# A conditioned mixer and 32 experts on one core: another order of weight loads, x scaled earlier, and products moved in TensorE's order

## The reference, cut to what matters

```
cond = silu(c)
mod = cond @ w_ada + b_ada
sh1, sc1, gt1, sh2, sc2, gt2 = split(mod, 6)
h = rms_norm(x, g_pre_mix) * (1 + sc1) + sh1
q, k, v, u, g_att, g_ssm = split(h @ w_in)
att = moba_attention(q, k, v, rel_bias) @ w_att_out
y = gelu(s5_ssm(u, ...))
glu_v, glu_g = split(y @ w_glu)
ssm = (glu_v * sigmoid(glu_g)) @ w_ssm_out
y = (sigmoid(g_att) * att + sigmoid(g_ssm) * ssm) @ w_out
x = x + gt1 * rms_norm(y, g_post_mix)
h = rms_norm(x, g_pre_ffn) * (1 + sc2) + sh2
x = x + gt2 * rms_norm(moe_ffn(h, ...), g_post_ffn)
```

## Time and profile before

| | |
|---|---|
| median of 3 runs | 1281.6 us (1278.81 to 1281.63) |
| the profiled execution, own time | 1276.95 us |
| its span | 1274.9 us |
| TensorE busy, share of the span | 1161.4 us, 91% |
| VectorE, ScalarE, GpSimd busy | 282.7, 166.4, 133.6 us |
| read from HBM | 463.72 MB |
| mean granted clock of TensorE | 0.955 |

### The profile page before, as it was taken

One profiled execution on the slowest core, in us unless ns is written; L12 is line 12 of the kernel. 1 busy time (PEld: TensorE's weight loads), 2 busy tenths in 40 slices (PEclk: granted clock), 3 DMA queues, 4 the chain that ended last, 5 costly groups with the idle time before them and its releaser, 6 DMA issues.

```text
span 1274.9 us, 16975 instructions
## 1 busy us (share of the span) xinstructions
PE 1161.4 (91%) x6973; PEld 593.1 (47%) x6973; DVE 282.7 (22%) x613; ACT 166.4 (13%) x360; POOL 133.6 (10%) x200
## 2 busy tenths in 40 slices
PE   5999999998999999989999899999799998899874
PEld 3665776856445444344543344443344442345332
DVE  3663784323210211101111111011002111011102
ACT  2201111202101111011011011011110110010001
POOL 4450776120000000000000000000000000000000
PEclk9998999997998999989999799999899999899887
DMA  9789434193899999999999999999999999999995
GB/s 350 249 315 353 165 129 171 66 388 132 363 379 422 419 422 422 420 421 404 421 420 421 421 421 414 420 421 420 420 415 416 420 421 421 420 414 421 420 421 238
DMA packets 88643, 465.93 MB, mean 365 GB/s; under 512 B 12451, under 2 KB 13608, under 8 KB 39412
## 3 DMA queue, kind: packets, MB, share of 16 engines
q1 hardware_dynamic: 86740, 460.27, 89.0%
q0 software_dynamic: 1568, 4.46, 1.1%
q10 hardware_dynamic: 256, 0.09, 0.0%
HBM read 463.72 MB, written 3.16 MB: 366 GB/s over the span
## 4 chain that ended last, share of the span: by engine, by line
PE 49%; SPq 30%; DMA 16%; issue 3%; DVE 1%; ACT 1%; ACTq 0%; POOL 0%; DVEq 0%; POOLq 0%
SPq L556 29%; DMA ring_w<-in_w_exp_out 10%; PE psum L762 9%; PE psum L1072 7%; PE psum L1175 4%; PE psum L1068 4%; PE psum L775 3%; PE psum L1077 3%; DMA ring<-in_w_ada 3%; PE psum L1004 2%; PE psum L1177 2%; PE psum L822 1%; PE psum L1209 1%; PE psum L1104 1%; PE psum L1207 1%
## 5 line engine op out<-in xcount | busy, mean ns | idle before, releaser
L1072 PE MATMUL psum<-ring_w,xe 128*64 128x512 f32 x960 | 210.6, 594 | 2.6 <-DMA ring_w<-in_w_exp_in 2.5
L1914 DVE TENSOR_SCALAR row_a<-psum 128x512 f32<-128x512 f32 (+1 forms) x37 | 22.1, 597 | 619.2 <-PE psum L1091 447.5
L1077 PE MATMUL psum<-ring_w,xe 128*32 128x256 f32 x1536 | 109.5, 432 | 37.8 <-DMA ring_w<-in_w_exp_in 34.2
L1072 PEld LDWEIGHTS psum<-ring_w,xe 128*64 128x64 f32 x960 | 67.0, 137 | 138.0 <-issue 128.0
L1177 PE MATMUL psum<-ring_w,aT 128*64 128x512 f32 x480 | 116.6, 609 | 5.0 <-DMA ring_w<-in_w_exp_out 4.5
L1068 PE MATMUL psum<-ring_w,xe 128*128 128x512 f32 x256 | 114.1, 598 | 3.9 <-DMA ring_w<-in_w_exp_in 3.9
L607 POOL TENSOR_SCALAR small<-small 128x1 f32<-128x1 f32 x6 | 1.5, 253 | 979.9 <-ACT row_g L1532 959.8
L1077 PEld LDWEIGHTS psum<-ring_w,xe 128*32 128x32 f32 x1536 | 49.4, 120 | 94.8 <-DMA ring_w<-in_w_exp_in 57.5
L762 PE MATMUL psum<-hT,ring 128*128 128x256 f32 x384 | 90.7, 393 | 1.6 <-DMA ring<-in_w_in 1.6
L1465 ACT ACTIVATE row_b<-row_a 128x512 f32<-128x512 f32 (+1 forms) x37 | 20.5, 554 | 535.2 <-DVE row_a L1914 535.2
L762 PEld LDWEIGHTS psum<-hT,ring 128*128 128x128 f32 x384 | 73.6, 195 | 16.2 <-issue 4.4
(11 more groups left out here) (312 smaller groups left out, 1026.5 us busy)
## 6 DMA issues: line engine op xcount, KB each, us to landing
ring_w<-in_w_exp_in SPq DMA_DIRECT2D x256, 1024.0 KB, 25.9
ring_w<-in_w_exp_out SPq DMA_DIRECT2D x128, 1024.0 KB, 26.5
ring<-in_w_ada SPq DMA_DIRECT2D x12, 2048.0 KB, 15.7
ring<-in_w_in SPq DMA_DIRECT2D x8, 2048.0 KB, 15.8
ring<-in_w_out SPq DMA_DIRECT2D x2, 2048.0 KB, 11.2
ring<-in_w_glu SPq DMA_DIRECT2D x1, 2048.0 KB, 7.9
ring<-in_w_att_out SPq DMA_DIRECT2D x1, 2048.0 KB, 8.3
ring<-in_w_ssm_out SPq DMA_DIRECT2D x1, 2048.0 KB, 10.4
```

What stands on the lines that cost most here:

```text
L1072: mm = pe.matmul(bank[b][64 * n:64 * n + 64, :], rows[:, k, :], w[:, FF * b + 512 * n:FF * b + 512 * n + 512], start=k == 0, stop=False, t ...
L1077: mm = pe.matmul(bank[0][32 * n:32 * n + 32, 256 * b:256 * b + 256], rows[:, k, :], w[:, FF * b + 256 * n:FF * b + 256 * n + 256], start=k ...
```

## The change

SP issues the mixer's blocks in an order of its own, ISSUE. Slots are still given by MIX, in which glu and ao change places. u comes as two transfers of 1 MB; the second is issued two blocks later and counts on another semaphore, which TensorE waits for before u's second half. ScalarE's squares of x, and VectorE's scalings, stand ahead of the parameters' chain. TensorE turns x before its first weight sum. The sums of sc1b and sh1b run inside u's first half, `inputs_to_states(0)` before the columns of sc2b, and wo0's first product waits for the merged pieces one by one.

```
-MIX = [..., "gt2a", "glu", "gt2b", "ao", "so", "wo0", "wo1"]
+MIX = [..., "gt2a", "ao", "gt2b", "glu", "so", "wo0", "wo1"]
+
+ISSUE = ["sc1a", "sh1a", "u", "sc1b", "sh1b", "u_rest", "q", "k", "gt1b", "gt1a", "sh2a", "v", "sc2a", "sh2b", "ga0", "sc2b",
+         "ga1", "gs0", "gs1", "gt2a", "ao", "gt2b", "glu", "so", "wo0", "wo1"]
...
-            for n, name in enumerate(MIX):
+            for name in ISSUE:
+                if name == "u_rest":
+                    sp.dma_start(slot(MIX.index("u") % MIX_SLOTS, 8)[:, 4:8, :],
+                                 source("u")[0][D // 2:D, :].rearrange("(k p) n -> p k n", p=P)).then_inc(stored, 16)
+                    continue
+                n = MIX.index(name)
...
-                if name == "sh2a":
+                if name == "sc2a":
                     sp.wait_ge(bias_out, 16)
...
+                if name == "u":
+                    sp.dma_start(slot(s, k)[:, 0:4, :], src[0:D // 2, :].rearrange("(k p) n -> p k n", p=P)).then_inc(slot_in[s], 16)
+                    continue
...
-            for name, s in (("ao", 1), ("so", 2), ("wo0", 3), ("wo1", 0)):
+            for name, s in (("glu", 1), ("so", 2), ("wo0", 3), ("wo1", 0)):
...
+                    if merged and k % 2 == 0:
+                        pe.wait_ge(merged_ready, k // 2 + 1)
...
-            ada_parts(0)
             for a in range(TT):
                 pe.wait_ge(normed, a + 1)
                 for k in range(KD):
+                    if a == 0 and k == 6:
+                        pe.wait_ge(vcol_ready, 1)
...
+            ada_parts(0)
             ada_columns(0)
...
                     for n in (2, 3):
-                        ada_parts(n)
                         ada_columns(n)
...
+                        if half == 0 and b == 1 and m == 1:
+                            ada_parts(2)
+                            ada_parts(3)
+                        if half and b == 0 and m == 0:
+                            pe.wait_ge(stored, 16)
...
             ada_parts(9)
+            inputs_to_states(0)
             ada_columns(9)
...
-            pe.wait_ge(merged_ready, 4)
...
-            for name in ("wo0", "wo1"):
-                tokens(name, 0, aoT)
+            tokens("wo0", 0, aoT, merged=True)
+            tokens("wo1", 0, aoT)
...
+            act.wait_ge(x_in, 16 * TT)
+            for n in range(TT):
+                act.activation(junk, xs[:, n, :], ACT.Square, accum_out=ss[:, n:n + 1]).then_inc(squares, 1)
+                act.wait_ge(squares, n + 1)
+
             act.wait_ge(vcol_ready, 1)
...
+            def normal(a):
+                dve.wait_ge(rstd_ready, a + 1)
+                ts(xs[:, a, :], xs[:, a, :], rstd[:, a:a + 1], None, ALU.mult).then_inc(normed, 1)
+
             dve.memset(b_rows, 0.0).then_inc(b_rows_clear, 1)
+            normal(0)
             dve.wait_ge(vec_in, 160)
...
             dve.tensor_copy(vcol, bank[3][:, 0:108]).then_inc(vcol_ready, 1)
+            normal(1)
```

More of the change, by code:

```diff
@@ L54 @@
 MIX = ["sc1a", "sh1a", "u", "sc1b", "sh1b", "q", "gt1a", "k", "gt1b", "v", "sh2a", "sh2b", "sc2a", "sc2b",
-       "ga0", "ga1", "gs0", "gs1", "gt2a", "glu", "gt2b", "ao", "so", "wo0", "wo1"]
+       "ga0", "ga1", "gs0", "gs1", "gt2a", "ao", "gt2b", "glu", "so", "wo0", "wo1"]
+ISSUE = ["sc1a", "sh1a", "u", "sc1b", "sh1b", "u_rest", "q", "k", "gt1b", "gt1a", "sh2a", "v", "sc2a", "sh2b", "ga0", "sc2b",
+         "ga1", "gs0", "gs1", "gt2a", "ao", "gt2b", "glu", "so", "wo0", "wo1"]
 ADA = ["sc1a", "sh1a", "sc1b", "sh1b", "gt1a", "gt1b", "sh2a", "sh2b", "sc2a", "sc2b", "gt2a", "gt2b"]
@@ L121 @@
 FILLS = []
-for name in MIX[:MIX.index("glu")] + ["ao", "glu", "so"]:
+for name in MIX[:MIX.index("gt2a")] + ["ao", "glu", "so"]:
     if name in ("glu", "ao"):
@@ L588, in _ @@
                 sp.dma_start(out[0, a * P:(a + 1) * P, :], xs[:, a, :]).then_inc(stored, 16)
-            sp.wait_ge(stored, 16 * TT)
+            sp.wait_ge(stored, 16 * TT + 16)
         @block.gpsimd
@@ L766, in features, with tokens @@
                 mm.then_inc(fill_done, 1)
-            def tokens(name, a, lhs):
+            def tokens(name, a, lhs, merged=False):
                 s = MIX.index(name) % MIX_SLOTS
@@ L915, in _ @@
             for h in range(HEADS):
-                inputs_to_states(h)
+                if h:
+                    inputs_to_states(h)
                 if 0 < h < HEADS - 1:
@@ L1334, in copy_ada @@
                 act.activation(ada_acc[:, n % 2, :], bank[ADA_BANK[n]], ACT.Copy).then_inc(ada_copied, 1)
[L1336 to L1339, removed]
             for half in range(2):
@@ L1577, in _ @@
             V.do(ts(x_scale_b, x_scale_b, 1.0, None, ALU.add))
-            for a in range(TT):
-                dve.wait_ge(rstd_ready, a + 1)
-                ts(xs[:, a, :], xs[:, a, :], rstd[:, a:a + 1], None, ALU.mult).then_inc(normed, 1)
             chain(tt(m1, rho, ec, ALU.mult))
```

## The result

The changed kernel takes 1271.8 us (median of 12 runs, 1267.8 to 1278.3), the kernel before, on the same chip, 1278.3 us (12 runs, 1274.2 to 1281.6). The ratio is 0.9956 [0.9938, 0.9974]: 5.6 us or 0.44% faster. The profiled executions differ by 5.9 us (own times 1271.08 and 1276.95). The ratios go by executions in the usual state; only one of those reported here was not, at 6416 us, of the kernel with gt1a second.

A forecast was written before the change was run, and what follows sets the result against it. The expert weights' stream bounds a rigid expert stage, so the mixer's gain decides: - 5.8 + 1.1 (sh2a's wait) + 5.2 + 4.8 + 1.5 = 6.8 us won, 1281.6 to 1274.8; range 1268 to 1282.

The forecast's parts named there:

- What bounds it: Expert stage: limited by the expert weights' stream and rigid, so the end moves one to one with the experts' order.
- Start and u in halves: Mixer's start: u at 24.3 instead of 26.21, 1.9 won; with u halved, 3 to 5 us won by q's first half.
- The new order of loads: Behind q: gt1a lands at 64.0, its sum 2.8 late, plus 3.0 of slow clock; 5.8 us lost by q's end.
- sc2b "about when wanted": Late mixer load: issued at v's end near 110, lands 8 later, about when wanted, as before; no term in the sum.
- The first heads: From last weight sum to the first head's product: 9.3 us instead of 14.5, 5.2 won, of which 3.08 is clock.
- ao, wo0: Late mixer: ao's 3.02 wait and slow group go, 4.8 won; wo0's 1.51 wait goes whole, 1.5 won.
- rival 1: gt1a less late, landing at 61.8, 2.4 lost; sum 10.2 won, 1271.4 us; chance 0.16.
- Rival 2: Clock takes most: gt1a at 65, 5 us lost clock, slow first head; 2.1 won, 1279.5; chance 0.24 with rival 4.
- Rival 3: Queue behind q runs at 254 GB/s, gt1a at 72 to 74; sum -3.2, 1284.8 us; chance 0.10.
- Rival 4: Waits move to other names, such as sc2b, without being removed; of rival 2's size; chance 0.24 with rival 2.

The follow-up runs named there:

- the kernel with gt1a second: The changed kernel with loads issued q, gt1a, k, gt1b instead of q, k, gt1b, gt1a: 0.9917 of the kernel before.
- the late scaling: Squares and scalings of x late as before: on the changed kernel 0.9974; on the one with gt1a second and sc2b ahead of ga0 0.9916.
- Writing by partition: Bias rows' write with 128 partitions outermost: with gt1a second 0.9873, the same with u as one transfer 0.9891, on the changed kernel alone 0.9952.
- the repeat: The changed kernel run again, unchanged: 0.9956 of the kernel before, its profiled execution 1276.6 us.
- gt1a third: The changed kernel with loads issued q, k, gt1a, gt1b instead of q, k, gt1b, gt1a: 0.9953 of the kernel before.
- sc2b ahead of ga0: The kernel with gt1a second, with sc2b issued before ga0 instead of after it: 0.9892 of the kernel before.

## Why the prediction was right

It forecast 6.8 us, 1274.8; measured are 5.6 us by the ratio and 5.9 between the profiled executions. The median of 1271.8 lies under the number because its base, 1281.6, was the median of three runs that lie high: twelve give 1278.3. The sum is close in part by luck: two terms were 3.5 us too good together (gt1a 1.9, sc2b 1.6), and 2.7 us of clock behind wo0, which no term had, made up for them in this trace.

**What bounds it.** Right. The order came 5.96 us earlier and the span ended 5.9 earlier. Over the mixer's experiments the time from the order to the last expert piece stayed between 941 and 944 us. It is not quite rigid: some 2 longer in seven of the thirteen traces, in six of which the first expert's product ran at the lower clock, so an edit ahead of it can lose up to 2 us there.

**Start and u in halves.** The start was right: u at 24.52 (24.3 forecast), 1.7 won of 1.9. Of u in halves less came out: sh1b's load landed at 34.3 and not at 33.1, which cost a wait of 1.19, u's second product, 8.83, took a slow spell, as allowed for, and q's first half ended at 58.4 (56 to 58). That is 2.3 us won up to there and not 3 to 5. That this gain is swallowed was the forecast's reason for not counting it, and the late scaling shows it from both sides: nothing lost in the trace with the 7 us wait (order 1.0 earlier), 1.57 of 1.80 lost without.

**The new order of loads.** The mechanism was right and two sizes were off. The bracket was 7.44 (6 to 8), and the clock behind it 2.87 (3.0 taken from rows that end at 3.08). gt1a came 4.7 late, not 2.8. The landings show why; the changed kernel's DMA issues of q, of q and k together (median), of gt1b and gt1a together, and of g_post_mix:

```profile
ring<-in_w_in SPq DMA_DIRECT2D x1, 2048.0 KB, 9.8
...
ring<-in_w_in SPq DMA_DIRECT2D x2, 2048.0 KB, 12.9
...
ring<-in_w_ada SPq DMA_DIRECT2D x2, 2048.0 KB, 18.3
...
row_g<-in_g_post_mix POOLq DMA_DIRECT2D x1, 512.0 KB, 7.3
```

q landed 1.2 later than taken (issued 0.75 later, and 9.8 instead of 9.3). k needed 6.7 behind it, gt1b and gt1a 5.4 and 5.3, which is the 5.4 of the prediction. The 1.3 more at k are g_post_mix: it took 7.3 beside the blocks, where it had landed in 4.1 with little beside it. The forecast took half of it (64.0 between 63.3 and 64.7); with all of it and q's 1.2, 65.9 is what came out, against 65.73. The Trainium skill ("DMA: Bandwidth & Descriptors", Issuing engines are not separate DMA queues) has the transfers of all issuers share the 16 engines; by this trace it is so, and whole. In four other runs with this order of loads gt1a landed between 63.7 and 64.7, so the changed kernel's trace is at the late end, and 64.0 was close to the usual one. What sets it is when q is issued, behind the small tables in SP's queue: at 37.14 to 38.54 us in these five traces, and gt1a's sum starts 26.7 to 27.3 us later in each. That a wait costs a slow clock behind it "each time" was read too widely: behind the waits of 1.14 and 1.51 in the earlier trace rows the products are at full speed (1.92 and 20.87), and the sum rightly put nothing there.

**sc2b "about when wanted".** This is the step that failed: it was put at nothing and cost 1.49 in the changed kernel and 3.89 once gt1a was in time. sc2b was issued at v's end, as forecast (111.6), but took 9.6 us to land, not 8. What was left out is the write of the bias rows ahead of it in the queue. The prediction has that write move behind v; it stood there before, and its new place is behind sh2a, as SP's queue of the kernel before shows:

```profile
70.44 0.37 SPq L550 DMA_DIRECT2D ring<-in_w_in  x1
70.85 0.78 SPq L539 DMA_DIRECT2D bias_rows<-bias_line  x1
71.68 33.92 SPq L550 DMA_DIRECT2D ring<-in_w_ada  x4
```

So it no longer delays sh2a (the 1.14 that went), but its packets now pass some 8 us later, from 84.5 to 97 instead of 76.5 to 90, in front of sc2a, sh2b, ga0 and sc2b. The prediction weighed it for its readers on VectorE (over 20 us of room) and not for these loads, while it left about half of the engines' time unused for its first 4 us. Writing by partition took the wait away on all three kernels on which it was tried.

**The first heads.** 5.1 for 5.2. But most of it is clock, and that term is less sure than it looks. From the last sum's start to the turned probabilities it was 16.3 us before, 11.2 in the changed kernel, 12.9 in three other traces with a bracket before sc2b, 15.8 in the repeat, and 17.0 with gt1a second (bracket 3.89). In the three traces in which neither sc2b nor ga0 waits it was 11.2 each time. The forecast's 9.3 (7.2 by VectorE's chain) came true: 125.05 + 7.15 - (121.22 + 1.92) = 9.06.

**ao, wo0.** 4.4 and 1.7 for 4.8 and 1.5. Undoing the exchange brought back 3.18 and 2.94 in the trace and 4.5 us in the ratio.

**The rivals.** The median, 1271.8, is next to rival 1's 1271.4, but the mechanism is not its: gt1a landed at 65.7 and not at 61.8, and the number comes from the base. As a kernel of its own, with gt1a second, rival 1 gives 0.9917. Rival 2's number for gt1a (65) was met, its slow first head came only in the changed kernel's repeat. Rival 3's queue at 254 GB/s did not come: behind q it ran at 386, and at 389 with gt1a third. Its row was misread, too: of the stretch from 70 to 80 the first 2 us are nearly empty (55 and 86 GB/s), v's load runs at 390 from 73, and the write's packets begin only at 76.5, with 222 GB/s to 80. Rival 4 came in small: sc2b has a wait that sh2a and ga0 had.

What stays open: how much each small edit is worth, since the clock's spells scatter one execution against another by 4 us and more; whether g_post_mix alone, issued elsewhere, would bring gt1a forward by 1.3, which wasn't tried, so its share in k's landing is argued from the times and not shown; and what the write by partition and sc2b ahead of ga0 would give together.

## What to carry to other kernels

When loads share one queue, set their order by when each is wanted and not by when its slot is free: a block that lands early in front of one that is wanted first turned a start 1.7 us earlier into a wait of 7.4. For each transfer that is moved, ask what stands behind it in the queue, not only who reads it, and look at the DMA engines' share while it runs alone: where it stays near a half, try the same bytes with another outermost count. Price a wait on TensorE with the clock that may fall behind it (0 to 3 us here), and don't judge an edit of 2 us by one trace.

## What the runs showed of the hardware

- A write of 2 MB with 8 as its outermost count kept the DMA engines at 0.4 to 0.5 for its first 4 us; the same bytes with 128 outermost kept them full and passed in 8 to 10 us instead of 11 to 12. Of its packets of 2 KB at most 53 passed in half a microsecond in the first form, and up to 102 in the second.
- One order of loads landed the same block between 63.7 and 65.7 us in five executions, following the issue of the first of them (37.14 to 38.54 us) at a nearly constant distance: the block's first product starts 26.7 to 27.3 us behind it.
- The granted clock's spells at the lower level (1.2 of 2.4 GHz) lasted from 3.4 to 13.7 us ahead of the experts, and the length of the wait ahead did not tell whether one comes. Before sc2b's sum, waits of 1.56, 1.68, 1.86 and 3.89 us were followed by a slow sum (3.20 to 3.64 us), one of 1.82 by a partly slow one (2.58) and one of 1.49 by a fast one (1.92); but before sh1b's sum waits of 1.83, 2.32, 2.86 and 3.31 left it fast (1.92 each), and one of 1.97 did not (3.62).
- Removing 7 us of wait did not shorten the kernel by 7: the changed kernel's 0.9956 became 0.9917, 5 us, until the next late load was cured as well (0.9873, 11 us in all).
